# Two of the four later conditioning columns of each layer, multiplied and added by VectorE

## The reference

```
mod = silu(c) @ w_ada[l] + b_ada[l]                  # 1024 x 6144, one row
sh1, sc1, gt1, sh2, sc2, gt2 = split(mod, 6)
h = rms_norm(x) * (1 + sc1) + sh1
pa, pb, pc, pd = split(h @ w_in[l])                  # four head groups
mix = concat(diff_attention(pa), neighborhood_attention(pb),
             conformer_conv(pc), dilated_attention(pd)) @ w_out[l]
x = x + gt1 * mix
h2 = rms_norm(x) * (1 + sc2) + sh2                   # the router and 32 experts read h2
x = x + gt2 * hier_moe(h2)
```

## Time and profile before

| | |
|---|---|
| profiled execution, its own time | 1795.89 us |
| its span, first to last instruction | 1794.1 us |
| median of the three runs | 1794.69 us |
| TensorE matmul busy | 1591.2 us (89%) |
| VectorE busy | 716.5 us (40%) |
| ScalarE busy | 433.9 us (24%) |
| GpSimd busy | 194.5 us (11%) |
| mean granted clock of TensorE | 0.97 of full speed |
| data moved | 528.47 MB, mean 295 GB/s |

### The profile page before, as it was taken

The page is one execution under the profiler, slowest core; times in us unless marked ns, Lnnn a source line. Parts: engine busy times, 40 slices in busy tenths (PEclk is TensorE's granted clock), DMA queues, the critical chain, the costliest instruction groups (busy, mean ns, idle before and its releaser), DMA issues. The chain is left out here.

```text
span 1794.1 us, 22384 instructions
## 1 busy us (share of the span) xinstructions
PE 1591.2 (89%) x7468; PEld 767.9 (43%) x7468; DVE 716.5 (40%) x1464; ACT 433.9 (24%) x987; POOL 194.5 (11%) x200
## 2 busy tenths in 40 slices
PE   5999999998998998888889999999899989878883
PEld 2455655463333333333345555455533333323331
DVE  1577476662222112122157855743522222222124
ACT  2111476111111112111121016741211111211112
POOL 0000022111111011111000002111110101101010
PEclk9999999989999999999999999999999989999997
DMA  9625533378999999999972365213899999999995
GB/s 360 236 71 188 211 115 111 145 296 335 405 398 404 408 404 401 413 409 412 362 295 94 114 215 195 82 48 108 305 403 398 402 411 404 404 414 403 398 409 197
DMA packets 124293, 528.47 MB, mean 295 GB/s; under 512 B 17184, under 2 KB 23328, under 8 KB 77568
## 3 DMA queue, kind: packets, MB, share of 16 engines
q1 hardware_dynamic: 106704, 491.50, 69.9%
q0 software_dynamic: 12480, 24.51, 4.3%
q10 hardware_dynamic: 4976, 10.55, 1.6%
HBM read 520.99 MB, written 23.86 MB: 304 GB/s over the span
## 5 line engine op out<-in xcount | busy, mean ns | idle before, releaser
L1405 PE MATMUL ps<-ring,arena 128*64 128x512 f32 x1728 | 498.9, 613 | 57.3 <-ACT arena L1693 30.4
L1405 PEld LDWEIGHTS ps<-ring,arena 128*64 128x64 f32 x1728 | 159.7, 141 | 290.1 <-issue 274.6
L1052 PE MATMUL ps<-ring,hT 128*128 128x512 f32 (+1 forms) x768 | 254.9, 487 | 3.5 <-DMA ring<-in_w_in 2.5
L739 DVE TENSOR_TENSOR arena<-ps,arena 64x512 f32<-64x512 f32 (+1 forms) x64 | 44.4, 693 | 460.5 <-ACT arena L1687 369.7
L1687 ACT ACTIVATE arena<-ps 128x512 f32<-128x512 f32 x64 | 38.2, 597 | 766.1 <-PE ps L1405 715.2
L1052 PEld LDWEIGHTS ps<-ring,hT 128*128 128x128 f32 x768 | 144.4, 191 | 103.4 <-issue 91.1
L747 DVE TENSOR_TENSOR arena<-ps,gate 64x512 f32<-64x512 f32 (+1 forms) x64 | 43.7, 683 | 288.1 <-PE ps L1405 268.1
L1017 POOL DMA_INDIRECT yexp_d<-arena,masks x64 | 59.3, 926 | 847.2 <-DVE arena L749 769.2
L1405 PE MATMUL ps<-home,arena 128*64 128x512 f32 x320 | 124.2, 606 | 13.6 <-ACT arena L1693 5.1
L1265 PE MATMUL ps<-ring,hT 128*128 128x512 f32 x256 | 112.5, 595 | 0.0
L1405 PE MATMUL ps<-work,arena 128*64 128x512 f32 x288 | 106.7, 595 | 5.8 <-ACT arena L1693 5.1
(11 more groups left out here) (232 smaller groups left out, 1767.7 us busy)
## 6 DMA issues: line engine op xcount, KB each, us to landing
ring<-in_w_exp_up SPq DMA_DIRECT2D x80, 1024.0 KB
ring<-in_w_exp_down SPq DMA_DIRECT2D x78, 1024.0 KB
ring<-in_w_exp_gate SPq DMA_DIRECT2D x74, 1024.0 KB
ring<-in_w_ada SPq DMA_DIRECT2D x24, 2048.0 KB, 10.8
ring<-in_w_in SPq DMA_DIRECT2D x8, 2048.0 KB, 21.7
home<-in_w_exp_gate SPq DMA_DIRECT2D x16, 1024.0 KB
hT<-in_w_exp_down SPq DMA_DIRECT2D x12, 1024.0 KB, 23.9
work<-in_w_exp_gate SPq DMA_DIRECT2D x12, 1024.0 KB
```

The lines of the kernel that those rows point to most:

```text
L739: dve.tensor_tensor(hid[0:w, :], ps[P - w:P, 1, :], sil[0:w, :], ALU.mult).then_inc(drained[1], 1)
L1052: last = pe.matmul(out, lhs(k), rhs(k), start=(k == 0), stop=(k == n - 1))
L1405: last = [pe.matmul(outs[c][HALF * c:HALF * c + HALF, :], lhs(k)[:, 0:HALF], rhs(c, k), start=(k == 0), stop=(k == n - 1), tile_position=( ...
```

## The change

Units 6 and 7 leave the list of steps at which TensorE multiplies. VectorE multiplies and adds their rows in group B's projections, unit 6 after it has copied qk tile 1 and unit 7 after qk tile 2; the sum is kept in the slot itself, in its first 512 columns. TensorE adds over the partitions at step 9 (unit 6) and step 11 (unit 7), ahead of `attend`, and VectorE's `mod_out` follows at the end of the same step. The slots are given back with these products and no longer with `ada`. Units 8 and 9 keep steps 12 and 29.

```diff
-ADA_STEPS = [1, 9, 12, 29]
+SUM_STEPS, ADA_STEPS = [9, 11], [12, 29]
 def ada_at(l, step):
-    return ADA_STEPS.index(step) if step in ADA_STEPS else None
+    return len(SUM_STEPS) + ADA_STEPS.index(step) if step in ADA_STEPS else None
+def sums_at(l, step):
+    return [ADA_LATER[l][SUM_STEPS.index(step)]] if step in SUM_STEPS else []
 # last_use
-                return l, "mod" if (l, u) in ADA_EARLY[l] else "ada", u
+                return l, "mod" if (l, u) in ADA_EARLY[l] + ADA_LATER[l][:len(SUM_STEPS)] else "ada", u
 # TensorE
+            def mod_of_sums(l, u):
+                key, w, p0 = (l, "mod", u), slot(UNIT["ada", l, u]), HALF * (u % 2)
+                pe.wait_ge(later_ready, len(SUM_STEPS) * l + ADA_LATER[l].index((l, u)) + 1)
+                await_free(pe, key)
+                for k in range(KD):
+                    last = pe.matmul(bank(key)[p0:p0 + HALF, k:k + 1], w[:, 0, k:512:KD], C["ones"],
+                                     start=True, stop=True, tile_position=(0, p0))
+                fills(last, key)
...
                         scores(i)
+                    for m, u in sums_at(l, i):
+                        mod_of_sums(m, u)
 # VectorE
+                def product_in_place(i):
+                    unit = UNIT[("ada",) + ADA_LATER[l][i]]
+                    sum_of_rows(unit, slot(unit)[:, 0, :], later_ready)
...
                             dve.sem_inc(rot_ready, 1)
+                            if 1 <= t <= len(SUM_STEPS):
+                                product_in_place(t - 1)
                             continue
...
+                    for m, u in sums_at(l, i):
+                        mod_out(m, u)
                     if ada_at(l, i - MOD_LAG) is not None:
                         mod_out(*ADA_LATER[l][ada_at(l, i - MOD_LAG)])
                     n = ada_at(l, i - 1)
                     if n is not None and turned_columns(*ADA_LATER[l][n]):
-                        if n >= 2:
-                            await_filled(dve, (ADA_LATER[l][n - 2][0], "mod", ADA_LATER[l][n - 2][1]))
                         ada_turned(*ADA_LATER[l][n], n % 2)
```

More of the change, by code:

```diff
@@ L260, in plan_banks @@
         for step in range(NSTEP):
+            for m, u in sums_at(l, step):
+                take((m, "mod", u), 7)
             if ada_at(l, step - MOD_LAG) is not None:
@@ L429, in program @@
         early_ready = sem("early_sum_ready")
+        later_ready = sem("later_sum_ready")
         next_ready = sem("next_sum_ready")
```

## The result

The changed kernel took 1800.28 us (median of 22 runs, 1794.86 to 1805.57), beside 1796.01 us for the kernel before on the same chip (22 runs, 1790.87 to 1801.36). The ratio is 1.0023, with a 95% interval of 1.0013 to 1.0032: 4.3 us slower by the medians, small but outside the measurement's noise. The forecast was 1795.8 us, within 0.1 us of no change from the profiled execution. The profiled execution after took 1803.88 us (before: 1795.89), a span of 1802.1 us and a mean clock of 0.968 (before: 0.970); it lies 3.6 us above the median, so not every microsecond read from it is in every run.

The account below looks back on a forecast made before the run. The bound depends on stage: TensorE in group B's projections, a chain from engine to engine in group A. 1795.89 - 1.3 (group D) + 1.2 (group A) = 1795.8 us; own range 1792 to 1799, whole range 1789 to 1803.

Parts of the forecast that it names:

- The sums on VectorE: Group B's projections: 6.0 us a unit hides in VectorE's waits for TensorE, 1.0 and 1.5 us left; cost 0.
- Rival 3: Group B's projections: sums don't fit between the tiles; at twice the price 19 us, 1815 us; chance 0.04.
- Group D: Steps 1 and 3: removing TensorE's work lets step 3's attending start earlier; gain 0.61 us, layer 1 0.65, together 1.3.
- Group A at full clock: Steps 9 and 11: 16 products take 2.06 us, delay step 9's chain, hidden at step 11; loss 0.6 a layer, together 1.2.
- The clock: Steps 9 to 12: as many falls to half clock as before, one; ends none (-3.2 us) and three more (+9.6).
- Rival 1: Steps 9 to 12: clock falls in the one-column products, 3.2 us a fall; 1799.0 to 1805.4 us; chance 0.22.
- a shorter wait would help: Step 12: TensorE's 1.52 us wait shrinks to about 0.3 us, which by the skill's idle-gap rule alone would help the clock.
- GpSimd's bias loads are in before: Load queue: later slot release moves next layer's loads back by up to 27 us without touching GpSimd's bias loads; cost 0.

Follow-up runs that it names:

- the sums alone: Kernel before, with VectorE's two sums added at the changed kernel's places, written to free memory and read by nobody: 1795.55 us, ratio 1.0000.
- the wait filled: Kernel before, with three products of 256 columns on constants added in TensorE's wait at step 12: 1792.65 us, ratio 0.9982.
- steps 10 and 11: Changed kernel, with unit 6's one-column products at step 10 instead of step 9: 1798.20 us, ratio 1.0025 to the kernel before.

## Why the prediction went as it did

**The sums on VectorE: right.** Forecast 6.0 us a unit with 1.0 and 1.5 us left over; measured 0.49 and 5.48, with 0.89 and 1.58 us left, TensorE's 48.56 us unchanged, and 1.0000 for the sums alone. Rival 3 is out.

**Group D: right.** Forecast 0.61 us; attending starts 0.68 us earlier, of which 0.07 is an earlier start of the stage (207.83 for 207.90). In layer 1, counted from the first scores, it is 0.67 for 0.65.

**Group A at full clock: right.** The 16 matmuls take 2.08 us. With 128 columns, which keep the clock, VectorE scales at 239.35 for 240.02; the stage starts 0.59 us earlier there (207.31), so the chain at step 10 is level: 0.6 us lost at step 9 less 0.6 gained in group D, as the sum had it. Over the long length the change with 128 columns is at 49.32 and 49.24 us, the kernel before with the wait filled at 49.47 and 49.44: 0.15 and 0.20 us a layer. The forecast was 1.3 - 1.2 = 0.1 us for both together, so the sum without the clock was right to 0.3 us.

**The clock: the step that failed.** The prediction said: "I take as many falls as before, one". The mis-sized term is that one. The profile shows four at these places, and the runs with 128 columns put the price of the one-column products at 0.38%, some 6.8 us; the kernel before pays some 3.2 us for its own falls (0.18%). With the rest of the sum near zero that leaves the change 6.8 - 3.2 = 3.6 us behind, near the 4.3 measured; both prices have intervals of some 2 to 3 us, and the 6.8 us hold whatever the meeting with GpSimd adds.

The row that decided was in hand: the clock fell in one-column products at 382.86, and the prediction said so, but set against it that "dense matmuls stand directly around each set of 16". That was no protection: 16 matmuls were enough, gapless, between full products, if not every time: in the profiles, half clock came with all eight one-column sets at step 11, with four of six at step 9 and neither of two at step 10, and with no set of 128 columns. Rival 1, held at 0.22, is what happened, between its times for one more fall (1799.0) and two (1802.2). By its own price the three more that the profile shows would have given 1805.4; but 3.2 us was the price of a stretch of 7.0 us at half clock, and a stretch of 3.6 us, as at step 9, cost less (1.48 us in layer 0 with steps 10 and 11, over 128 columns at the same steps). The time lies outside the forecast's own 1792 to 1799, and inside 1789 to 1803 only because that range took rival 1 in; the sum does not give it. Half clock around steps 9 to 12 in both layers was one of the prediction's own signs of being wrong, and it is there.

The second half of that step, that a shorter wait would help, came about in part (forecast 0.3 us; 0.57 for 1.52 in layer 0, 1.25 in layer 1) and was of no use, for what filled the wait lowered the clock as well.

The rule in the Trainium skill, "TensorE: Matmul & The Clock Gate", section "HAM oscillation — how this bites in real kernels", is told of idle gaps in TensorE's work, and the gaps of its example are longer than those here. By it the products, which leave no gap, would have cost nothing. That idle time matters agrees with the filled wait, though it was only 1.52 us (0.9982); the fall with steps 10 and 11 came behind no idle time at all, so there the measurement decides against the rule.

**Missed: GpSimd.** The prediction found that "GpSimd's bias loads are in before" and looked no further; the tables' arithmetic behind those loads meets the mix when the mix comes late or early by some tenths of a us. In the profile after the held-up operations are 1.84 us longer in layer 0 and 2.30 in layer 1, together 4.14 of the 8.55 us lost there. The clock costs its price without it (128 columns at step 9 alone: 2.88 and 3.07 us with no meeting), and 128 columns at step 11 alone is near the run with both although its profile has the meeting in both layers. But no run has the whole loss over the kernel before and a profile without the meeting, so how often it happens in the timed runs, and its share of the 4.3 us, stay open.

**Where the time of the profile went.** Layer 0, 5.67 us: 2.96 from step 12 to 16 by the clock (14.49 for 11.53), 1.84 in the two held-up VectorE operations of step 10, and the rest, 0.87, at step 9 by the clock, where ScalarE's reciprocal sums came at 240.51 for 239.64. Layer 1, 2.88 us: steps 12 to 16 are 0.21 us shorter than before (both had a fall there), and 3.09 us are lost ahead of them: 2.30 in the held-up mix and coefficient, and the rest, 0.79, where the fall at step 9 stands.

## What to carry to other kernels

A TensorE product with one moving column has a price beyond its 2 us: what runs behind it may run at half clock, even with no gap between, though it need not. Where only a sum over partitions is wanted, 128 columns of ones cost the same time here and keep the clock; and a wait of 1.5 us in the middle of dense work was worth filling with a product that nobody reads. When a change shifts an engine by half a microsecond, look at what GpSimd does in memory beside VectorE just then, and when judging a version that gained, give the same clock care to the kernel before: it left no gain that could be measured here.

## What was not expected of the hardware

- 16 matmuls of 128 x 64 weights take 2.08 us with one moving column and 2.19 us with 128; the columns were not what took the time.
- The granted clock fell to 0.50 behind 16 gapless one-column matmuls, at steps 9 and 11 and in both layers of the profile after, and stayed at full behind the same 16 with 128 columns in every profile. With one column at step 10 it stayed at full too.
- A VectorE operation on 128 x 1 numbers took 1.30 us for 0.22, and one on 128 x 512 took 2.37 us for 0.75, beside GpSimd's operations of two inputs, 1.78 us each; beside one of one input a mix kept its 0.75 us (240.67 in the kernel before). Whether VectorE or GpSimd gives way varies: with 128 columns in both, VectorE's mix kept its 0.75 us and GpSimd's operation took 2.27 for 1.77.
